# The last two units of three projections taken by token block, and VectorE's low halves moved behind the first norm

## The reference, cut to what matters

```
for i in range(DEPTH):
    z = x @ w_in[i]                                   # q, k, v, u and two gates
    merged = sigmoid(g_attn) * (a_out @ w_branch_attn[i]) + sigmoid(g_ssm) * (s_out @ w_branch_ssm[i])
    x = layer_norm(DEEPNORM_ALPHA * x + merged @ w_out[i], ln1_g[i], ln1_b[i])
    ffn = swiglu(x, ...) if i % 2 == 0 else moe_swiglu(x, ...)
    ple = jax.nn.sigmoid(x @ ple_w_gate[i]) * (p[i] @ ple_w_proj[i])
    x = layer_norm(DEEPNORM_ALPHA * x + ffn + ple, ln2_g[i], ln2_b[i])
```

## Time and profile before

| | us |
|---|---|
| median of 3 runs (lowest to highest) | 1717.13 (1716.88 to 1719.39) |
| the profiled execution | 1716.71 |
| its span | 1714.9 |
| TensorE busy in it | 1608.3 |
| VectorE busy in it | 1379.2 |
| ScalarE busy in it | 988.5 |

### The profile page before, as it was taken

How to read it: one execution, slowest core, us unless ns; L and a number is a source line. 1 busy time by engine, 2 the same in 40 slices (tenths; PEclk the granted TensorE clock), 3 DMA queues, 4 the chain that set the end, 5 groups by cost and what they waited for, 6 DMA issues and landing times.

```text
span 1714.9 us, 24273 instructions
## 1 busy us (share of the span) xinstructions
PE 1608.3 (94%) x9080; PEld 1361.9 (79%) x9080; DVE 1379.2 (80%) x1324; ACT 988.5 (58%) x845; POOL 69.4 (4%) x101
## 2 busy tenths in 40 slices
PE   7997899999798788999999999999999999999995
PEld 5886779998697676788788788788788788788884
DVE  8974765554988476898898998998998898998996
ACT  3233334344544333676776776776776677676772
POOL 4050010000200000000000000000000000000000
PEclk9998999999899799999999999999999999999998
DMA  7532766553233175799999999999999999999991
GB/s 243 168 100 73 268 204 211 183 196 110 75 123 124 50 277 185 264 381 345 338 370 346 333 369 345 339 368 345 336 368 345 339 371 338 338 372 344 338 375 49
DMA packets 217714, 456.46 MB, mean 266 GB/s; under 512 B 7910, under 2 KB 60167, under 8 KB 217144
## 3 DMA queue, kind: packets, MB, share of 16 engines
q1 hardware_dynamic: 216888, 450.91, 74.3%
q0 software_dynamic: 768, 4.75, 0.8%
HBM read 453.01 MB, written 2.62 MB: 266 GB/s over the span
## 4 chain that ended last, share of the span: by engine, by line
PE 82%; DVE 9%; ACT 3%; issue 3%; DMA 2%; POOL 0%; DVEq 0%; SPq 0%; ACTq 0%; POOLq 0%
PE psum L575 18%; PE psum L577 18%; PE psum L576 18%; PE psum L582 5%; PE psum L584 5%; PE psum L583 5%; PE psum L625 5%; DVE wl L395 2%; PE psum L953 2%; PE psum L972 1%; DMA ring<-in_w_out 1%; ACT wh L389 1%; ACT ring_split L389 1%; DVE ring_split L395 1%; PE psum L1021 1%
## 5 line engine op out<-in xcount | busy, mean ns | idle before, releaser
L395 DVE TENSOR_TENSOR wl<-ring,wh 128x2048 fp32r<-128x2048 f32 x379 | 860.7, 2290 | 155.4 <-ACT wh L389 151.5
L389 ACT ACTIVATE wh<-ring 128x2048 fp32r<-128x2048 f32 x379 | 728.2, 1924 | 192.3 <-PE psum L577 147.7
L575 PE MATMUL psum<-wh,xgh 128*128 128x512 f32 x896 | 356.2, 398 | 7.5 <-DVE wl L395 6.1
L577 PE MATMUL psum<-wh,xgl 128*128 128x512 f32 x896 | 349.8, 390 | 0.0
L576 PE MATMUL psum<-wl,xgh 128*128 128x512 f32 x896 | 348.9, 389 | 0.0
L575 PE MATMUL psum<-wh,hidh 128*128 128x512 f32 x536 | 210.2, 392 | 3.8 <-DVE hidl L1877 2.2
L577 PE MATMUL psum<-wh,hidl 128*128 128x512 f32 x536 | 209.5, 391 | 0.0
L576 PE MATMUL psum<-wl,hidh 128*128 128x512 f32 x536 | 209.2, 390 | 0.0
L575 PEld LDWEIGHTS psum<-wh,xgh 128*128 128x128 f32 x896 | 168.2, 188 | 46.9 <-DVE wl L395 9.7
L577 PEld LDWEIGHTS psum<-wh,xgl 128*128 128x128 f32 x896 | 168.2, 188 | 36.3
L576 PEld LDWEIGHTS psum<-wl,xgh 128*128 128x128 f32 x896 | 168.5, 188 | 31.9
(11 more groups left out here) (360 smaller groups left out, 2073.7 us busy)
## 6 DMA issues: line engine op xcount, KB each, us to landing
ring<-in_moe_gu SPq DMA_DIRECT2D x224, 1024.0 KB, 7.0
ring<-in_moe_dn SPq DMA_DIRECT2D x112, 1024.0 KB, 6.9
ring<-in_w_in SPq DMA_DIRECT2D x26, 1024.0 KB, 5.4
ring<-in_w_gu SPq DMA_DIRECT2D x22, 1024.0 KB, 5.1
ring<-in_w_dn SPq DMA_DIRECT2D x11, 1024.0 KB, 5.0
ring<-in_w_out SPq DMA_DIRECT2D x8, 1024.0 KB, 6.6
ring<-in_w_pg SPq DMA_DIRECT2D x8, 1024.0 KB, 5.1
ring<-in_w_ba SPq DMA_DIRECT2D x4, 1024.0 KB, 5.1
```

The costliest lines, as they stand in the source:

```text
L389: eng.activation(parts(u)[0], ring[:, ring_slot(u), :], ACT.Copy).then_inc(hi_ready, 1)
L395: eng.tensor_tensor(lo, ring[:, ring_slot(u), :], hi.bitcast(F32), ALU.subtract).then_inc(lo_ready, 1)
L575: pe.matmul(dst, ah, bh, start=first, stop=False, skip_group_check=True)
L577: return pe.matmul(dst, al, bh, start=False, stop=last, skip_group_check=True)
```

## The change

In the output projection the last two units are taken together by token block: both units' matmuls for b = 0, then `o_full`, then both units' for b = 1. Each unit's `unit_used` comes with its part for b = 1. The same is done to the last two units of the dense mixer's `down`; for that the last lap of TensorE's loop is written out behind it. On VectorE the low half of U + 1 moves from before the norm of block 0 to behind it. In the dense mixer's tail the low halves of the first two units of layer 1 move from before both norms to one behind each.

```
-                for i in range(4):
+                def project_out(i, b):
+
                     pe.wait_ge(lo_ready, split_index(u + i) + 1)
                     pe.wait_ge(m_lo, KD * l + 2 * i + 2)
...
+                for i in range(2):
+                    project_out(i, 0)
+                    project_out(i, 1).then_inc(unit_used, 1)
+                project_out(2, 0)
+                project_out(3, 0).then_inc(o_full, 1)
+                for i in (2, 3):
+                    project_out(i, 1).then_inc(unit_used, 1)
...
-                    with pe.Fori(1, FSTEPS // 2) as m:
+                    with pe.Fori(1, FSTEPS // 2 - 1) as m:
...
-                    u += (FSTEPS // 2 - 1) * 6
-                    down(u, 0, 0, FSTEPS, last=True)
-                    u += 1
+                    u += (FSTEPS // 2 - 2) * 6
+                    up(u, 0, 1, FSTEPS - 3)
+                    down(u + 2, 0, 0, FSTEPS - 2)
+                    up(u + 3, 0, 0, FSTEPS - 2)
+                    u += 5
+                    down_block(u, 0, 1, FSTEPS - 1, 0)
+                    down_block(u + 1, 0, 0, FSTEPS, 0, last=True).then_inc(o_full, 1)
+                    down_block(u, 0, 1, FSTEPS - 1, 1).then_inc(unit_used, 1)
+                    down_block(u + 1, 0, 0, FSTEPS, 1, last=True).then_inc(unit_used, 1)
+                    u += 2
...
-                make_lo(dve, U), make_lo(dve, U + 1)
+                make_lo(dve, U)
...
                     if b == 0:
-                        make_lo(dve, U + 2)
+                        make_lo(dve, U + 1), make_lo(dve, U + 2)
...
-                    make_lo(dve, LAYER_UNITS), make_lo(dve, LAYER_UNITS + 1)
...
                         layer_norm(1, xa, xa, b)
+                        make_lo(dve, LAYER_UNITS + b)
```

More of the change, by code:

```diff
@@ L826, in by_token_halves @@
                         mm.then_inc(unit_used, 1)
-                for i in range(4):
+                def project_out(i, b):
                     pe.wait_ge(lo_ready, split_index(u + i) + 1)
                     pe.wait_ge(m_lo, KD * l + 2 * i + 2)
[L831 to L838, removed]
+                    for k in range(2):
+                        for o in range(2):
+                            mm = product(bank[OUT_BANKS[2 * b + o]], mTh[:, 2 * i + k, b * P:(b + 1) * P],
+                                         mTl[:, 2 * i + k, b * P:(b + 1) * P], u + i, 2, k, o * 512, 512,
+                                         i == 0 and k == 0, i == 3 and k == 1)
+                    return mm
+                for i in range(2):
[5 more added lines that the diff above has]
+                    project_out(i, 1).then_inc(unit_used, 1)
                 u += 4
@@ L900, in up, with down_block, down @@
                             mm.then_inc(unit_used, 1)
-                    def down(s, lap, par, ready, first=False, last=False):
+                    def down_block(s, lap, par, ready, b, first=False, last=False):
                         pe.wait_ge(h_ready, ready)
                         pe.wait_ge(lo_ready, split_index(s) + 1 + lap)
+                        for k in range(2):
+                            for o in range(2):
+                                t = k * SEQ + b * P
+                                mm = product(bank[OUT_BANKS[2 * b + o]], hidh[:, par, t:t + P], hidl[:, par, t:t + P], s, 2, k,
+                                             o * 512, 512, first and k == 0, last and k == 1)
+                        return mm
+                    def down(s, lap, par, ready, first=False):
                         if first:
                             pe.wait_ge(pg_th, 2)
[L908 to L916, removed]
+                        down_block(s, lap, par, ready, 0, first)
+                        down_block(s, lap, par, ready, 1, first).then_inc(unit_used, 1)
                     up(u, 0, 0, None)
```

## The result

The changed kernel is slower: 1725.27 us (median of 6 runs, 1723.7 to 1728.95) beside 1718.09 for the kernel before in the same session (1716.88 to 1722.1). The ratio is 1.0040, with a 95% interval of 1.0028 to 1.0053, so 4.8 to 9.1 us. Measured again in a later session it was 1.0052 (1.0034 to 1.0071). The profiled execution took 1728.1 us, with a span of 1726.3; it is among the slower ones.

A forecast was written before the change was run, and what follows sets the result against it. It took VectorE's queue as the path at the changed places, with TensorE behind it moving the end. Terms 0.0 + 2.0 + 2.6 + 1.0 - 0.1, plus 0.1 for written-out code, gave +5.6: 1722.3 us, range 1719.8 to 1725.5.

The forecast's parts named there:

- Layer 0, VectorE's queue: Layer 0's output projection: VectorE's queue stays as long, so block 1 and the start of U + 1 don't move; 0.0 us.
- The clock behind it: Behind layer 0's projection: TensorE's longer hole drops the clock, so U + 1 starts slow; +2.0 us, 0 to 3.0.
- The tail's queue: Dense mixer's tail: VectorE idles for o_full, then makes low halves on the path; +2.6 us.
- The tail's clock: Dense mixer's tail: a 4.3 us TensorE hole may halve the clock for o_full's 12 matmuls; +1.0 us.
- The written-out lap: Dense mixer: writing out the last lap of TensorE's loop costs little; 0.1 us in the sum.
- Layer 1's projection: Layer 1's output projection: router's wait goes (-0.4), clock stays low longer (+0.3); -0.1 us, between -0.6 and +1.
- Rival (a): Layer 0's projection and mixer's tail: the clock never falls at either new place; +2.5 us, 1719.2; chance 0.18.
- (c): Both projections and the tail: the norms' earlier start reaches the end; -5.5 us, 1711.2; chance 0.07 with smaller gains.
- the case that I had put at 1723.3: Layer 0's projection and mixer's tail: both clock losses at full price; +6.6 us; within the forecast's joint chance of 0.66.
- Rival (d): Mixer's tail: its 2.6 us is given back in layer 1's holes, clocks as before; 1717.0; chance 0.09.

The follow-up runs named there:

- tail_pe: Only TensorE's block order and written-out lap in the dense mixer's tail changed, VectorE's order as before, against the kernel before; ratio 1.0007.
- tail_dve: Only VectorE's order in the dense mixer's tail changed (two low halves behind the norms), against the kernel before; ratio 1.0030.
- tail_only: Both halves of the change in the dense mixer's tail, output projections as before, against the kernel before; ratio 1.0022.
- proj_pe: Only TensorE's block order in the two output projections changed, VectorE's order as before, against the kernel before; ratio 1.0002.
- proj_dve: Only VectorE's order in the two output projections changed, TensorE's units one after the other, against the kernel before; ratio 1.0037.
- late_lows_tail_warm: late_lows plus twelve matmuls that nobody reads in the mixer's tail; ratio 0.9956 to the kernel before, 1712.4 beside 1717.3 us.
- late_lows: Against the kernel before: projections with TensorE's new blocks and low halves behind second norm and last xTl; tail's second low half behind last xIl; ratio 0.9973.

## Why the prediction was right, and where its sizes were off

- **Layer 0, VectorE's queue: 0.0.** Right: block 1 starts 14.16 us behind low U in both kernels, U + 2's high half (211.57, ready 213.5) held nobody up, as forecast, since VectorE's pair of low halves ran without a hole (from 212.18, the second at 214.4).
- **The clock behind it: 2.0, of 0 to 3.0.** The mechanism was right and the size low: 1.67 and 1.92 in the two profiles behind U + 1's start. What I had left out are the transposes of block 1 at half clock and ScalarE's copies behind them, +0.70 in both. The clock fell 2.1 us after TensorE stopped, ahead of the transposes, so it cost them too. That U + 1 starts at full clock in the kernel before is more than the luck of one run: of the five profiles with the projection of before it fell there in one (tail_pe, 204.82).
- **The tail's queue: 2.6.** 2.5, in tail_dve, where the 12 matmuls ahead of `o_full` ran at full clock; the transposes behind the norms were at half clock in both kernels.
- **The tail's clock: 1.0, an even chance of 2.** It fell in every profile with the hole of 4.34 us unfilled (four of four), for 1.4 to 1.6 us with VectorE's new order, and only 0.45 with the old. The 1.0 was an average of two cases of which only the costly one came.
- **The written-out lap: 0.1.** U + 1 to V takes 203.26 us with it (tail_only) and 203.27 without (before), both at full clock.
- **Layer 1's projection: -0.1.** The router's wait went (-0.49 from low U to the router), and from the router on 0.78 was added by a longer stretch at half clock: +0.3. In the second profile block 1's transposes were at half clock as well, and the two came to +0.22 and +0.66: +0.9, still inside the -0.6 to +1. The forecast reads the last window of rows 4 as half clock at 653.8; its mean clock is 1.00, and the half clock began just behind it, from 653.8 to 657.2.

The sum of the path's terms in the first profile is 0.70 + 1.67 + 4.11 + 0.29 = 6.8 us, against 5.6 forecast; the measured ratios are 6.9 and 8.9 us. Of the 11.4 us between the two profiles the other 4.6 lie in stretches whose code is the same: 0.45 ahead of the branch products, 1.1 from there to low U, 1.4 in layer 1's mixers and 1.7 in the experts. The last is the clock (3.4 us at half clock from 712.3); that from the branch products to low U was 41.4 to 41.7 us in the changed kernel and 40.5 before. Versions with TensorE's blocks in the projection had 39.8 to 42.4 and those without 39.7 to 40.7, which may be chance or a real microsecond; it is not explained here. So the forecast had the mechanisms and ran low by 1.2 us on the path. That the first measurement lies so near it is in part chance: in the second the median was 1727.5 beside 1717.3, above the 1725.5 where the forecast's range ends.

Rival (a), the clock never falls, and (c), the norm's early start gains, are refuted: both new places lost the clock, the case that I had put at 1723.3; (c) by block 1's start and by proj_pe and proj_dve. Rival (d) fails as well: layer 1 gave nothing back. As the Trainium skill says ("TensorE: Matmul & The Clock Gate", "What's actually happening"), the count of slow matmuls at a start varies from run to run; these runs agree, with 5.8, 7.4 or 8.6 us for the same 48 matmuls of layer 1 (below). The runs of one kernel scatter over 5 to 12 us here, and the correlation with the granted clock above says that most of it is the clock.

## What to carry to other kernels

Moving work behind a wait pays only if the wait's own engine has something else to do: ask what fills the wait afterwards, and count the moved work again where it lands. A step that releases an engine earlier than it can be used only moves its idle time to a longer hole, and on TensorE a longer hole has a price of its own. What shortens such a path is taking work behind the last result that the bound engine waits for, not behind an intermediate one.

## What the runs showed of the hardware

- A hole of 3.1 us ahead of the same 48 matmuls of layer 1 cost the clock in 7 of the 14 profiles and left it in 7. The 48 matmuls took 5.8 us in these, 7.3 to 7.4 in four of the others, where half clock lasted 3.4 us, and 8.5 to 8.6 in three, where it lasted 6.8. I had counted 3.1 us as safe from the one profile of before.
- Eight transposes (1.1 us) between two holes did not always hold the clock: in the kernel before, layer 1, they ran at 2.4 GHz between waits of 2.38 and 1.57 us, and the clock fell at 653.8 as TensorE went on. Nor did they bring it back in the changed kernel, where it had fallen before them in layer 0 and stayed at half until 3.7 us behind U + 1's start. At 1.2 GHz the eight take 1.97 us instead of 1.10.
- Twelve matmuls that nobody reads, put between dependent norms, kept TensorE at 2.4 GHz through a tail in which the clock fell in the twelve other profiles (two profiles have the twelve matmuls): 0.7 us less in late_lows_tail_warm than in late_lows from V to layer 1 and, in that profile, 3.5 us less from there to the router (202.2 and 198.7). That this alone makes the kernel faster is not shown by the ratios, whose intervals overlap.
- The time from the start to the state branch's first product (the row of L733) was 129.0 to 129.9 us in ten profiles and 131.4 to 132.4 in four, with the same code. This too is the clock: those four, and no other, have 3.4 us at half clock between 24 and 38 us. TensorE had no wait there, so a hole was not needed for it. A window of late_lows holds 10 matmuls in 4 us of a busy engine, where the same window of the kernel before holds 19 at a clock of 1.00:

```profile
33.00:37.00 4.00, 4.00 (x10) 2.83 (x9) 3.94 (x8) 3.76 (x8) 2.46 (x6) 0.57 1.07 382
```
